# Expert weights read as 8 KB runs per partition, with gathered rows and gated products in permuted columns

## What is computed

```python
g_logits = xt @ w_rg + b_rg                       # (T, 4)
e_logits = xt @ w_re + b_re                       # (T, 32)
...
hb = jax.nn.silu(xb @ w1[e]) * (xb @ w3[e])       # xb: rows of expert e; w1, w3: 1024 x 512
return hb @ w2[e]                                 # w2: 512 x 1024
...
out = x + sum over the two experts of weight * y
```

## Time and profile before

| | before |
|---|---|
| median of 3 runs | 1998.66 us (1998.25, 1998.66, 2004.2) |
| span of the profiled execution | 2003.3 us |
| PE busy | 1795.4 us, 90% of the span |
| DVE busy | 1042.8 us, 52% |
| ACT busy | 849.2 us, 42% |
| DMA queue q1 (SP's) | 183120 packets, 339.46 MB, 47.7% of 16 engines' span |
| mean granted clock of TensorE | 0.949 of 2.4 GHz |

### The profile page before, as it was taken

The page is one execution under the profiler, slowest core; times in us unless marked ns, Lnnn a source line. Parts: engine busy times, 40 slices in busy tenths (PEclk is TensorE's granted clock), DMA queues, the critical chain, the costliest instruction groups (busy, mean ns, idle before and its releaser), DMA issues. The chain is left out here.

```text
span 2003.3 us, 23200 instructions
## 1 busy us (share of the span) xinstructions
PE 1795.4 (90%) x8735; PEld 1400.6 (70%) x8735; DVE 1042.8 (52%) x1125; ACT 849.2 (42%) x863; POOL 97.5 (5%) x106
## 2 busy tenths in 40 slices
PE   4999999999999999999988989649999999999980
PEld 3788888879868878676666889436666666666650
DVE  4343535342214121366664241268878878888866
ACT  5333333422122220144542021227777777777751
POOL 2100000000000000000000000010000000000005
PEclk9999999999999999799998989859999999999995
DMA  5631313133322334334414230569999999999927
GB/s 175 188 126 52 126 52 126 42 126 120 133 84 70 103 126 149 104 123 149 148 42 152 84 127 21 205 212 361 379 378 374 375 376 375 372 376 373 368 98 262
DMA packets 195259, 382.26 MB, mean 191 GB/s; under 512 B 11401, under 2 KB 70865, under 8 KB 191121
## 3 DMA queue, kind: packets, MB, share of 16 engines
q1 hardware_dynamic: 183120, 339.46, 47.7%
q0 software_dynamic: 8384, 29.63, 4.7%
q10 hardware_dynamic: 3712, 12.62, 1.6%
HBM read 314.02 MB, written 67.65 MB: 191 GB/s over the span
## 5 line engine op out<-in xcount | busy, mean ns | idle before, releaser
L1470 DVE TENSOR_TENSOR e_l<-e_raw,e_h 128x2048 fp32r<-128x2048 f32 x192 | 439.3, 2288 | 113.8 <-ACT e_h L1464 111.9
L1464 ACT ACTIVATE e_h<-e_raw 128x2048 fp32r<-128x2048 f32 x192 | 364.6, 1918 | 75.6 <-PE ps L1486 49.6
L193 PE MATMUL ps<-uh,w_h 128*128 128x512 f32 x1024 | 320.4, 394 | 20.5 <-DVE ul L844 12.8
L193 PE MATMUL ps<-ul,w_h 128*128 128x512 f32 x1024 | 318.6, 393 | 0.0
L193 PE MATMUL ps<-uh,w_l 128*128 128x512 f32 x1024 | 318.3, 392 | 0.0
L177 DVE TENSOR_TENSOR w_l<-w_raw,w_h 128x2048 fp32r<-128x2048 f32 x40 | 91.6, 2291 | 355.5 <-ACT w_h L173 355.5
L193 PEld LDWEIGHTS ps<-uh,w_h 128*128 128x128 f32 x1024 | 194.4, 190 | 62.5 <-issue 21.9
L1486 PE MATMUL ps<-e_h,e_xth 128*96 128x512 f32 x512 | 208.9, 408 | 30.4 <-DVE e_xtl L1571 30.4
L193 PEld LDWEIGHTS ps<-ul,w_h 128*128 128x128 f32 x1024 | 194.7, 190 | 41.3
L193 PEld LDWEIGHTS ps<-uh,w_l 128*128 128x128 f32 x1024 | 194.2, 190 | 40.8
L1486 PE MATMUL ps<-e_h,e_xtl 128*96 128x512 f32 x512 | 203.0, 397 | 0.0
(11 more groups left out here) (250 smaller groups left out, 2220.6 us busy)
## 6 DMA issues: line engine op xcount, KB each, us to landing
e_raw<-w_exp_gate SPq DMA_DIRECT2D x64, 1024.0 KB, 6.2
e_raw<-w_exp_up SPq DMA_DIRECT2D x64, 1024.0 KB, 7.7
e_raw<-w_exp_down SPq DMA_DIRECT2D x64, 1024.0 KB, 6.4
w_raw<-w_in SPq DMA_DIRECT2D x28, 1024.0 KB, 5.6
qk_d<-qk SPq DMA_DIRECT2D x16, 1024.0 KB, 4.1
at_qk<-qk_d SPq DMA_DIRECT2D x8, 2048.0 KB, 8.9
y_d<-e_y ACTq DMA_DIRECT2D x32, 384.0 KB, 6.0
y_d<-zeros POOLq DMA_DIRECT2D x22, 384.0 KB, 10.8
```

The lines of the kernel that those rows point to most:

```text
L193: mm = pe.matmul(ps[:, h * HALF:(h + 1) * HALF], w[:, k, :], u[:, k, h * HALF:(h + 1) * HALF], start=first, stop=last)
L1464: act.activation(self.e_h[m % SPLIT][:, :, :], self.e_raw[slot][:, :, :], ACT.Copy).then_inc(self.e_hi[m % SPLIT], 1)
L1470: dve.tensor_tensor(self.e_l[slot][:, :, :], self.e_raw[slot][:, :, :], self.e_h[m % SPLIT][:, :, :].bitcast(F32), ALU.subtract).then_inc( ...
```

## The change

Which row of a weight matrix lies in which partition is changed for all router and expert weights: partition p holds rows (number of chunks) times p + k instead of row 128k+p. So a half of gate or up is, in each partition, four neighbouring rows of 512 (8 KB in one run), and a half of down two neighbouring rows of 1024 (8 KB). The contraction index is permuted alike on the other side: DVE writes `rt_xn` so that column 128k+p holds channel 8p+k, and `e_hid` so that column 128k+p holds hidden channel 4p+k. Both are written with a step of 128 elements between neighbouring elements of the inner loop and read in order. The transposes read as before.

The halves of down no longer are column halves but halves of the contraction: a new function `down_products` makes for each of two chunks the three products in each of the two banks of `ps_y`, 12 matmuls per piece as before; two neighbouring ones have the same stationary operand and different banks. Both banks are finished with the second piece. The router weights get the same order of rows; their tile and the number of their elements are unchanged.

```diff
-                rows = lambda w: w[0].rearrange("(k p) n -> p k n", p=P)
+                rows = lambda w: w[0].rearrange("(p k) n -> p k n", p=P)
...
-                        dve.scalar_tensor_tensor(out=xn[b][:, :], in0=k_.x2[:, bass.ds(t, 1), :].rearrange("p a n -> p (a n)"),
-                                                 scalar=rstd[:, bass.ds(t, 1)], in1=g_b[:, :], op0=ALU.mult,
+                        by_lane = lambda row: row.rearrange("t (p k) -> t p k", k=KD)
+                        dve.scalar_tensor_tensor(out=xn[b][:, :].rearrange("t (k p) -> t p k", p=P),
+                                                 in0=by_lane(k_.x2[:, bass.ds(t, 1), :].rearrange("p a n -> p (a n)")),
+                                                 scalar=rstd[:, bass.ds(t, 1)], in1=by_lane(g_b[:, :]), op0=ALU.mult,
                                                  op1=ALU.mult).then_inc(scaled, 1)
...
-        w = self.ins["w_exp_" + kind][0][e].rearrange("(k p) n -> p k n", p=P)
-        src = w[:, :, half * HALF:(half + 1) * HALF] if kind == "down" else w[:, 4 * half:4 * half + 4, :]
+        w = self.ins["w_exp_" + kind][0][e].rearrange("(p k) n -> p (k n)", p=P)
         slot, _ = self.raw_slot(piece)
-        eng.dma_start(self.e_raw[slot][:, :, :], src).then_inc(self.e_in[slot], 16)
+        eng.dma_start(self.e_raw[slot][:, :, :].rearrange("p k n -> p (k n)"), w[:, 4 * HALF * half:4 * HALF * (half + 1)])\
+            .then_inc(self.e_in[slot], 16)
...
+    def down_products(self, pe, ps, ht_h, ht_l, piece, half):
+
+        j, b, m = piece
+        slot, _ = self.raw_slot(piece)
+        pe.wait_ge(self.e_lo[m % SPLIT], 2 * j + m // SPLIT + 1)
+        w_h, w_l = self.e_h[m % SPLIT], self.e_l[slot]
+        for k in range(2):
+            at = 2 * half + k
+            for x, w, first, last in ((ht_h, w_h, at == 0, False), (ht_h, w_l, False, False), (ht_l, w_h, False, at == 3)):
+                for c in range(2):
+                    mm = pe.matmul(ps[:, c * HALF:(c + 1) * HALF], x[:, at, :], w[:, 2 * k + c, :], start=first, stop=last)
+        mm.then_inc(self.e_used[m % SPLIT], 1)
...
-            k_.piece_products(pe, ps_y[:, half * HALF:(half + 1) * HALF], ht_h, ht_l, piece, True, True)
+            k_.down_products(pe, ps_y, ht_h, ht_l, piece, half)
...
-            dve.tensor_tensor(hid[:, :], silu[:, :], ps_u, ALU.mult).then_inc(hid_out, 1)
+            by_lane = lambda row: row.rearrange("t (p k) -> t p k", k=4)
+            dve.tensor_tensor(hid[:, :].rearrange("t (k p) -> t p k", p=P), by_lane(silu[:, :]), by_lane(ps_u), ALU.mult)\
+                .then_inc(hid_out, 1)
```

## The result

The changed kernel takes 2012.63 us (median of 20 runs), the kernel before 1998.68 us in the same comparison (20 runs): a ratio of 1.0065, 95% interval 1.0048 to 1.0082, so 10 to 16 us slower. The prediction was 1998.2 us, no change that can be measured. The measured time lies inside its range of 1993 to 2022 us, but on the side of rival A, and clear of no change.

What follows compares the result with a forecast made beforehand. PE's ring through ACT was taken to bound the expert stage, with loads hidden. Terms -0.5 + 0 + 0 + 0 = -0.5 us off the median of 1998.7 gave 1998.2 us, range 1993 to 2022.

Steps and rivals of the forecast that it cites:

- rival A: `e_hid` in the expert stage, `rt_xn` in the route stage: stepped writes cost up to 23.2 us (17.5 + 5.7), chance 0.18.
- What bounds the kernel: Expert stage: PE's work and late `e_xtl` set 18.92 us per expert; loads near the DMA ceiling but hidden; `e_hid` without slack.
- the ring: Expert round: ACT's next copies start when down ends, so PE time lost from 1618.34 to down's end recurs in 32 experts.
- Loads of 8 KB runs: Weight loads: DMA share falls from 1.04 to between 0.92 and 1.0, worth 0 in the expert stage.
- The 0.5 us in the route stage: Two weight pieces ahead of the stores of `xn_d` on SP's queue land sooner: 0.5 us off, bounds -0.6 and 0.
- `e_hid` written with steps: DVE's 32 writes in the expert stage: cost taken as 0, upper bound 547 ns each, 17.5 us in all.
- the double pace: Upper bound for DVE's stepped writes: each element takes twice its time, 547 ns more per `e_hid`.
- Down's order: Down's matmuls in the expert stage, neighbours sharing the stationary operand: taken as 0, bounds -3.8 us and 0.
- Rivals B and C: B: all 72 matmuls per expert gain, 11.5 us faster, chance 0.05; C: 8 KB runs load slower, 65 us, chance 0.03.
- Rival D: Weight loads: runs cut back into 2 KB packets, share stays 1.04, time 1998.7 us; counted within the forecast's case.

Runs made afterwards that it cites:

- `hid_only`: Kernel before plus the stepped `e_hid`, down's rows permuted to match, its 2 KB runs and column halves kept: ratio 1.0050, 31 rounds 593.9 us.
- `hid_early`: Changed kernel with `e_hid` moved ahead of the low part of piece 5 in DVE's order: ratio 1.0003 to the kernel before, 31 rounds 584.7 us.
- the late kernels: ACT's copy and store of finished rows moved later, `e_hid` earlier: on kernel before 0.9862, on changed kernel 0.9909, with 8 KB gate/up, 4 KB down 0.9832.
- the bench: Kernel before with single DVE and ACT instructions, stepped and unstepped, at the head of the last stage: 31 rounds 582.3 us, total not judged.

## Why the prediction was wrong

*What bounds the kernel*: right. Nothing waited for loads, and `e_hid` had no slack, as `hid_only` and `hid_early` show; the late kernels show the ring. (From 1350 to 1900 us the page's row for DVE before has 7 or 8 in each slice, not "8 or 9". Nothing rests on it.)

*Loads of 8 KB runs*: right as to the packets, the share (0.99 to 1.00, at 366 to 369 GB/s, since the rounds were longer) and a worth of nothing in the stage. The 0.5 us in the route stage can't be told from its spread.

*`e_hid` written with steps*: this step failed. I took 0 between bounds of 0 and 547 ns, because two rows showed no cost. It measured 375 ns, which made 11.6 us of rounds when it was the only part changed. Neither row could show that price. L300 has its steps in PSUM, where the bench finds no cost with steps of 2, 4 and 8. L315 has 8 elements and one source. With one source the bench gives (225 - 196) / 64 = 0.45 ns per element, an estimate of 3.6 ns for eight, and rows as short as this scatter by more. The next line of the kernel before is a second stepped write of the same shape and step, which the prediction leaves out when it calls L315 the only one (duration ns min/median/max, first and last start us):

```profile
L316 DVE TENSOR_SCALAR prm<-na_eq x1: 167/167/167, 13.8 to 13.8; 128x8 f32<-128x8 f32 x1
```

It takes 167 ns, 4 ns less than L1332 without a step. So these rows spoke against the double pace, 8 to 9 ns, but not against less than half of that. The nearest rows were near in name only. What the Trainium skill says of lines was the better guide, and 0.18 for rival A too little.

*Rival A*: the right mechanism, its price too high. `e_hid` took 375 ns more, not 547; times 32 that is 12.0 us of the 17.5. In the 31 rounds it is 11.6 us, and 10.4 after the 1 us from down's order. `rt_xn` took 703 ns more, not 1094, and cost nothing instead of 5.7 us: DVE's time in it grew by 5.3 us and its idle time before it fell by 4.4 us (19.2 to 14.8), the waits for stores of `xn_d` alone from 9.8 to 4.3 us, so most of the longer write took the place of a wait. The point from which the prediction would have it decide, 0.19 us per `e_hid`, was passed twofold.

*Down's order*: in its bounds; 0.9 us of the 3.8 came. *Rivals B and C*: not seen; the matmuls of gate still start 0.231 us apart (ten from 1819.31 to 1821.62), and 8 KB runs load faster. *Rival D*: refuted by the packets.

The 2.6 us between the rounds' 10.4 and the total's 13 are within its interval.

## What to carry to other kernels

A permutation that makes DMA runs long can be paid on the other side by an engine that walks SBUF with steps: look whether neighbours still share 16 bytes (a step of 2 float32, or pairs), and if not, whether that engine's instruction is on the path. Longer runs are worth their DMA time only where something waits for a load; here that began when a ring through ACT was shortened, and then 8 KB runs for gate and up and 4 KB runs for down were worth 6 us. A row used as evidence that something is free must have the same memory, the same number of sources and enough elements to show the price asked of it.

## What the runs showed of the hardware

- DVE, float32, 512 elements, two sources: 691 ns in order, 693 with a step of 2, 842 with 3, 1062 with 4, 1081 with 8; a stepped read costs the same as a stepped write, to within 8 ns. A stepped source in SBUF together with one in PSUM costs `e_hid` no more than a stepped write (1054 and 1052 ns); two stepped operands in SBUF were not run. A chunk pitch of 528 instead of 512 bytes changes 1052 to 1043 ns.
- ACT: 632 to 1129 ns with a step of 4, 0.97 ns per element on top, more than DVE's 0.72.
- PSUM reads by DVE and ACT: no cost with a step of 8 elements (291 and 278 ns for 128 elements either way).
- PE's load of a stationary operand (96x128, float32): 141 and 143 ns in order, 214 with a step of 4 elements, 202 with 8.
- Alone, 2 KB runs load 384 to 389 GB/s at a share of 1.04 to 1.05, 8 KB runs 414 to 434 at 0.99 to 1.04 (windows of 2 us from 1306 to 1320).
